# Seven-product feed-forward layers: 16 of 22 units cut, VectorE's second weight sum and gated product each one piece later

## The reference

```python
D_FF = -(-8 * D_MODEL // (3 * 256)) * 256      # 2816, that is 22 chunks of 128
def swiglu(x, w_gu, w_down):
    g, u = jnp.split(x @ w_gu, 2, axis=-1)
    return (jax.nn.silu(g) * u) @ w_down
...
h = h + swiglu(rms_norm(h, ffn_norm[layer]), ffn_w_gu[layer], ffn_w_down[layer])
```

## Time and profile before

| what | value |
|---|---|
| time, median of 3 runs | 2204.48 us (2204.3 to 2204.71) |
| the profiled execution: its time | 2204.36 us |
| its span in the trace | 2202.6 us |
| PE busy | 2166.3 us, 98% |
| DVE busy | 1304.2 us, 59% |
| ACT busy | 1015.8 us, 46% |
| first product stage of ffn0 | 504.85 to 577.15 us, first matmul of down |
| second product stage of ffn0 | 643.16 to 745.15 us, first matmul of down |

### The profile page before, as it was taken

How to read it: one execution, slowest core, us unless ns; L and a number is a source line. 1 busy time by engine, 2 the same in 40 slices (tenths; PEclk the granted TensorE clock), 3 DMA queues, 4 the chain that set the end, 5 groups by cost and what they waited for, 6 DMA issues and landing times.

```text
span 2202.6 us, 31009 instructions
## 1 busy us (share of the span) xinstructions
PE 2166.3 (98%) x11970; PEld 1819.5 (83%) x11970; DVE 1304.2 (59%) x1910; ACT 1015.8 (46%) x1516; POOL 308.2 (14%) x255
## 2 busy tenths in 40 slices
PE   8999999999999999999999999999999999999998
PEld 6888888789889888877898898878777778888887
DVE  6655656378658643554696486466576555555522
ACT  5445555345324434565453253355566554444312
POOL 0211112220000120003200000300010043222211
PEclk9999999999999999999999999999999999999999
DMA  3311111122323322201223223321221232222221
GB/s 139 115 58 39 56 41 39 58 96 77 117 83 108 115 96 77 96 20 53 83 80 131 77 99 132 134 91 44 72 73 39 72 111 95 101 95 95 96 96 58
DMA packets 31664, 184.79 MB, mean 84 GB/s; under 512 B 3105, under 2 KB 7713, under 8 KB 11313
## 3 DMA queue, kind: packets, MB, share of 16 engines
q1 hardware_dynamic: 29520, 175.42, 22.5%
q0 software_dynamic: 2016, 7.60, 1.1%
HBM read 178.78 MB, written 7.37 MB: 85 GB/s over the span
## 4 chain that ended last, share of the span: by engine, by line
PE 92%; DVE 4%; ACT 2%; issue 1%; DMA 0%; SPq 0%; POOL 0%; DVEq 0%; POOLq 0%; ACTq 0%
PE ps L2288 25%; PE ps L2290 25%; PE ps L2289 25%; PE ps L2618 2%; PE ps L3106 1%; PE ps L2612 1%; PE ps L3089 1%; PE ps L3049 1%; PE ps L2881 1%; PE ps L3116 1%; PE ps L2921 1%; PE ps L2639 1%; DVE wl L1221 0%; DVE sq L1977 0%; DMA raw<-in_stream 0%
## 5 line engine op out<-in xcount | busy, mean ns | idle before, releaser
L2288 PE MATMUL ps<-xh,wh 128*128 128x512 f32 (+1 forms) x1608 | 620.9, 386 | 3.3 <-POOL xl L2238 2.1
L2290 PE MATMUL ps<-xh,wl 128*128 128x512 f32 (+1 forms) x1608 | 595.1, 370 | 0.0
L2289 PE MATMUL ps<-xl,wh 128*128 128x512 f32 (+1 forms) x1608 | 593.9, 369 | 0.0
L1221 DVE TENSOR_TENSOR wl<-raw,wh 128x2048 fp32r<-128x2048 f32 x108 | 250.7, 2321 | 239.9 <-ACT wh L508 239.9
L2288 PEld LDWEIGHTS ps<-xh,wh 128*128 128x128 f32 x1608 | 303.6, 189 | 57.8 <-issue 11.9
L2290 PEld LDWEIGHTS ps<-xh,wl 128*128 128x128 f32 x1608 | 302.7, 188 | 53.2
L2289 PEld LDWEIGHTS ps<-xl,wh 128*128 128x128 f32 x1608 | 303.7, 189 | 47.6 <-issue 4.3
L508 ACT ACTIVATE wh<-raw 128x2048 fp32r<-128x2048 f32 x108 | 206.4, 1911 | 241.3 <-PE ps L2290 241.0
L2288 PE MATMUL ps<-part_h,wh 128*128 128x512 f32 x512 | 201.9, 394 | 0.5
L2290 PE MATMUL ps<-part_h,wl 128*128 128x512 f32 x512 | 200.6, 392 | 0.0
L2289 PE MATMUL ps<-part_l,wh 128*128 128x512 f32 x512 | 199.8, 390 | 0.0
(11 more groups left out here) (416 smaller groups left out, 3811.7 us busy)
## 6 DMA issues: line engine op xcount, KB each, us to landing
raw<-in_stream SPq DMA_DIRECT2D x158, 1024.0 KB, 4.8
hankd<-tabd SPq DMA_DIRECT2D x1, 3072.0 KB, 17.2
hank<-hankd POOLq DMA_DIRECT2D x4, 768.0 KB, 5.1
hT<-in_xT SPq DMA_DIRECT2D x4, 512.0 KB, 6.6
keepd<-hT POOLq DMA_DIRECT2D x1, 2048.0 KB, 9.9
hT<-keepd POOLq DMA_DIRECT2D x8, 256.0 KB, 4.8
out<-hT SPq DMA_DIRECT2D x8, 256.0 KB, 2.6
raw<-in_stream SPq DMA_DIRECT2D x2, 512.0 KB, 8.2
```

What stands on the lines that cost most here:

```text
L1221: dve.tensor_tensor(wl[:, s, :], raw[:, s, :], wh[:, s, :].bitcast(F32), ALU.subtract).then_inc(lo_made, 1)
L2288: pe.matmul(out, w_hi, a_hi, start=start, stop=False)
L2289: pe.matmul(out, w_hi, a_lo, start=False, stop=False)
L2290: return pe.matmul(out, w_lo, a_hi, start=False, stop=stop)
```

## The change

Both layers cut six units more in all, three each: the first stage has one uncut unit of its seven (5) in place of two (5 and 9), the second none of its ten in place of two (15 and 19). 16 of the 22 units of a layer are cut, before 13. The lists of skips (slots passed over) are new, so that the last piece of a unit and the following whole unit meet the slots that they need.

In the walk of the pieces, VectorE makes wsum[1] (second_operand) behind the low part of piece 1 and not ahead of it. The gated product of a unit stands one step later (p - 2 in place of p - 1), hidden on ScalarE one step later (p - 3 in place of p - 2), and hidden_lo on VectorE one step later (p - 4 in place of p - 3).

```diff
--- before.py
+++ after.py
@@ -109,7 +109,7 @@
 FAST = ("ffn0", "ffn1")
 PLAIN, CUT = 5, 12
 TOK = SEQ // 2
-GROUPS = ((PLAIN, CUT, "PSSSPSS", (20,)), (CUT, FC, "SSSPSSSPSS", ()))
+GROUPS = ((PLAIN, CUT, "PSSSSSS", (12, 13, 22, 23, 32, 33)), (CUT, FC, "SSSSSSSSSS", (30, 31)))
 CUTS = {n: kind == "S" for first, _, kinds, _ in GROUPS for n, kind in enumerate(kinds, first)}
 SEVENS = [n for n, cut in CUTS.items() if cut]
 QUARTERS = (7, 8, 9, 10)
@@ -656,7 +656,7 @@
 
                 def products(first, last):
                     order = pieces_of(first, last)
-                    for p in range(len(order) + 2):
+                    for p in range(len(order) + 3):
                         if p + LEAD < len(order):
                             hi(*order[p + LEAD])
                         n, k = order[p - 1] if 0 < p <= len(order) else (None, None)
@@ -664,12 +664,13 @@
                             copy_out(n)
                         elif k == 8:
                             silu_whole(n)
-                        n, k = order[p - 2] if p > 1 else (None, None)
+                        n, k = order[p - 2] if 1 < p <= len(order) + 1 else (None, None)
                         if k == 1:
                             silu_left(n)
                         elif k == 5:
                             silu_right(n)
-                        elif k in LAST:
+                        n, k = order[p - 3] if p > 2 else (None, None)
+                        if k in LAST:
                             hidden(n)
                         if p == len(order) - 3:
                             act.wait_ge(*piece_done(f, *order[-5]))
@@ -1419,7 +1420,7 @@
                     dve.wait_ge(operand_hi, fast_count(operand_hi, f, 3 * kc + 3))
                     dve.tensor_tensor(t_l[:, :, kc, :], t_sum, t_h[:, :, kc, :].bitcast(F32), ALU.subtract).then_inc(operand_lo, 1)
 
-                def first_sums(n):
+                def first_sum(n):
                     u, i = fast_unit(name, n), 4 * SEVENS.index(n)
                     q = [raw[:, u % 2, SEQ * j:SEQ * j + SEQ] for j in range(4)]
                     dve.wait_ge(raw_landed[u % 2], 16 * (u // 2) + 16)
@@ -1429,6 +1430,10 @@
                     else:
                         dve.wait_ge(operand_lo, fast_count(operand_lo, f, 12))
                     dve.tensor_tensor(wsum[:, 0, :], q[2], q[3], ALU.add).then_inc(weights_summed, 1)
+
+                def second_operand(n):
+                    u, i = fast_unit(name, n), 4 * SEVENS.index(n)
+                    q = [raw[:, u % 2, SEQ * j:SEQ * j + SEQ] for j in range(4)]
                     dve.wait_ge(weights_summed, fast_count(weights_summed, f, i + 1))
                     dve.tensor_tensor(wsum[:, 1, :], wsum[:, 0, :], q[0], ALU.subtract).then_inc(weights_summed, 1)
 
@@ -1455,12 +1460,14 @@
 
                 def operand(n, k):
                     if k == 1:
-                        first_sums(n)
+                        first_sum(n)
                     elif k == 2:
                         difference(n)
                     elif k == 3:
                         last_sum(n)
                     lo(n, k)
+                    if k == 1:
+                        second_operand(n)
 
                 def gate_left(n):
                     dve.wait_ge(prod_done, fast_count(prod_done, f, COUNT[n, 1]))
@@ -1494,7 +1501,7 @@
 
                 def products(first, last):
                     order = pieces_of(first, last)
-                    for p in range(len(order) + 3):
+                    for p in range(len(order) + 4):
                         if p + LEAD < len(order):
                             operand(*order[p + LEAD])
                         if p == len(order) - 3:
@@ -1512,10 +1519,10 @@
                             gate_right(n)
                         elif k == 6:
                             up_left(n)
+                        n, k = order[p - 2] if 1 < p <= len(order) + 1 else (None, None)
+                        if k in LAST:
                             gated(n)
-                        elif k == 10:
-                            gated(n)
-                        n, k = order[p - 3] if p > 2 else (None, None)
+                        n, k = order[p - 4] if p > 3 else (None, None)
                         if k in LAST:
                             hidden_lo(n)
```

## The result

| | before | after |
|---|---|---|
| time, median (runs) | 2204.6 us (4) | 2224.26 us (4), 2222.55 to 2225.24 |
| ratio, 95% interval | | 1.0089, 1.0076 to 1.0102 |
| profiled execution: time, span | 2204.36, 2202.6 us | 2225.24, 2223.4 us |
| mean granted TensorE clock | 0.999 | 0.994 |

Slower by 0.89%, where 2212.0 us (slower by 0.34%) was forecast: the direction holds, the time lies 6 us above the range.

What follows compares the result with a forecast made beforehand. TensorE, busy 98% of the span, was taken as the bound; per layer, longer waits of 4.05 and 2.6 us less 2.9 saved gave + 3.75, + 7.5 for two layers: 2212.0 us, range 2206.5 to 2218.

Steps and rivals of the forecast that it cites:

- The clock: Rival: TensorE's clock falls behind two stage-end waits (+ 3 us) or all four (+ 6), 2215 to 2219 us; chance 0.14.
- the forecast's own waits: TensorE waits before the down products: 4.4 us at each first stage end, 2.95 at each second.
- The prediction's last sign of being wrong: Granted TensorE clock behind the stage-end idles drops below 1.00 for long.
- VectorE's step: VectorE's time per cut unit: 10.28 us, between 10.1 and 10.46, falling 0.31 us behind TensorE each unit.
- The wait of 0.29 us for ScalarE: VectorE's wait within today's cut unit; moving ScalarE's copy behind silu_left should take most of it away.
- The chains at the stage ends: Product, silu_left, copy, split_hi, split_lo, then gate_right (first end) or hidden low part (second): waits 4.4 and 2.95 us.
- The bank shift: First stage end: with 44 results for 39, bank 4 holds (11, 5), so the down product waits for gate_right.
- TensorE's 9.97 us: Cut unit takes TensorE 9.97 us against 10.94 uncut, saving 2.9 us per layer, 5.8 in all.
- (d): Rival: TensorE runs dry inside the stages from late transfers or waits for ScalarE, + 1 to + 4 us more; chance 0.09.
- the margin at (11, 3): Thinnest place inside the first stage: piece made by 569.4, taken by TensorE at 570.2, 0.8 us left.
- (c): Rival: VectorE's time per cut unit comes down to 9.97 us; 2204.6 us, at best 2200.6; chance 0.15.

Runs made afterwards that it cites:

- experiment 2: Changed kernel with ScalarE's high part of the whole unit one step earlier, ahead of silu_left and hidden of the stage's last units: 2205.71 us, ratio 1.0006.
- experiment 3: Kernel before with the three moves in the operation order alone, still 13 cut units: 2208.76 us, ratio 1.002.
- experiment 4: Kernel before with the new table of 16 cut units alone, old order of VectorE's and ScalarE's operations: 2225.83 us, ratio 1.0093.
- experiment 6: Changed kernel with the whole unit's high part earlier on ScalarE and the bank rotation begun at bank 2 instead of 4: 2202.74 us, ratio 0.9993.
- experiment 9: Kernel before, with each down product's first matmul waiting for the stage's last hidden chunk, not the last but one: 2224.56 us, ratio 1.009.
- experiment 10: Changed kernel with ScalarE's high part for piece 1 of the next unit made ahead of silu_left and hidden: 2218.74 us, ratio 1.0062.
- experiment 11: Changed kernel with the bank rotation begun at bank 2 instead of 4, nothing else: 2221.81 us, ratio 1.0079.
- experiment 7: Changed kernel with the first weight sum made by GpSimd and not by VectorE: 2246.29 us, ratio 1.0189.
- experiment 8: Changed kernel with the whole unit's high part earlier, banks from 2, and the first weight sum on GpSimd: 2224.35 us, ratio 1.009.
- experiment 12: Changed kernel with the whole unit's high part earlier, banks from 2, and the next unit's piece 1 high part ahead of silu_left and hidden: 2199.15 us, ratio 0.9975.
- experiment 5: Changed kernel with 20 and 14 extra matmuls of ones on TensorE in the waits behind first and second stages: 2214.42 us, ratio 1.0046.
- experiment 1: Changed kernel with 36 and 24 extra matmuls of ones on TensorE behind the first and second stages: 2224.58 us, ratio 1.0091.

## Why the prediction was wrong

**The clock: the step that failed.** The sum had no term for it. It stood as a rival, 0.14, with 1.4 us per wait or up to twice that (1.5 to 2.9 were measured, so its price was about right), "against it that the new waits are shorter than 4.97, those of the second stage by 2 us". The start of the program is one case of an idle time that brings the lower clock, and I read its length as if it were a bound. It is none. The waits at the stage ends in the profiled runs of before, of the changed kernel and of experiments 2, 3, 4, 6, 9, 10 and 11, and what the slow steps behind them cost:

| wait, us | slow behind it | lost, us |
|---|---|---|
| 0.27 to 1.37 (14 waits) | none | 0 |
| 2.21 to 2.51 (6 waits) | two | 1.5, 1.6 |
| 3.43 to 3.66 (8 waits) | seven | 1.3 to 1.6 |
| 3.82 to 4.46 (6 waits) | all | 1.5 to 2.9 |
| 5.06, 5.08 | both | 2.7, 2.9 |

The four waits of experiment 7 (4.00 to 5.06 us) were all followed by slow steps too, those of 8 and 12 (1.38 at most) by none. Priced by this table, the forecast's own waits cost 3 to 9 us of clock: those of 4.35 us 1.5 to 2.9 each, those of 2.85, for which there is no row, 0 to 1.6 each. That is 2215 to 2221 instead of 2212. The falling clock was the likeliest case and not a rival. In the changed kernel it is 8.7 us in the trace, and experiment 5 shows that it goes when TensorE does not idle. The prediction's last sign of being wrong, the granted clock below 1.00 behind the idles, is the one that came. The Trainium skill, TensorE: Matmul & The Clock Gate, section Why this matters for your kernels, was cited for this and given too little weight; the trace agrees with it on every wait above 3.5 us. The page's limit for such gaps lies above two waits that were followed by slow steps here (2.41 and 2.51 us) and below one that was not (3.43); there the measurement decides.

**VectorE's step: a term mis-sized.** Taken as the middle of 10.1 and 10.46, which was a choice and no measurement; measured 10.39. The wait of 0.29 us for ScalarE went, as argued. But the low part of piece 1 now stands between the sums, and waits 0.13 us for its own high part, which ScalarE makes behind silu_left and hidden; another 0.16 stays before the low part behind up_left. Experiment 10 takes the first away. The first step of the first stage is longer still, 10.62 (523.80 to 534.42), with a wait of 0.31 us for ScalarE's high part at 529.67. The product of the last unit but one comes at 573.08 and not 572.3, and the waits are 5.07 and 3.62 (means of the two layers) where 4.35 and 2.85 were forecast: 3.0 us over four ends. So of the 13.3 us between the 2211.9 computed for the profiled execution and its 2225.24, 8.7 are the clock, 3.0 VectorE's lateness, and the rest lies where nothing was changed (see the ledger).

**The chains at the stage ends: right.** From split_lo's start to the down product 4.49 us (4.45 forecast), last waited gate_right at the first end; at the second end the hidden low part ends at 753.20, 0.22 before the down product starts (the trace names fork, right ahead of it). What the prediction did not say of them is how much of it was order: the high part of the whole unit behind silu_left and the copy costs 2.6 to 2.9 us at each end (experiment 2).

**The bank shift: right**, 1.1 to 1.2 us at each first end (experiment 11). **TensorE's 9.97 us: right**, ten units in 99.84 us (99.8 forecast). **Running dry inside the stages, (d): right that it hardly happens**, the margin at (11, 3) was used up to a gap of under 0.1 us. **VectorE keeps up, (c)**: not in the changed kernel. In experiment 12 its step of 10.24 is still above 9.97, but what it falls behind by no longer reaches TensorE at the second ends, since the other two parts of the waits are gone. Its 2199.15 us lie under the 2200.6 that (c) called the best the change can do, for (c) kept the order of the stage end as it was.

## What to carry to other kernels

Price a new wait of TensorE twice: its length, and the matmuls behind it at half clock, which in these runs cost 1.3 to 2.9 us more behind some waits of 2.4 us and behind all above 3.5; a clock that never falls in the trace of before says nothing on this when that trace has no such wait. A change that loads the second engine nearer to the first is paid where the pipeline drains: look there for the one operation in the wrong place of an in-order queue before giving up the saving. And an idle engine is not free help when its work slows the one that is full: time one operation of each side by side first.

## What the runs showed of the hardware

- The clock's answer to waits of equal length differs: of two waits of 2.51 and 2.47 us in one execution one was followed by slow steps, of four of 3.43 to 3.52 us three were. The times scatter accordingly: 2204.14 to 2208.13 us over eleven runs of experiment 2, 2198.09 to 2199.93 over nine of experiment 12. That the scatter is the clock's was not traced run by run.
- The slow steps need not begin with the first matmul: in the changed kernel the second down product starts at 753.42, four matmuls go at the full pace, and the slow steps run from 754.42 to 757.79.
- Matmuls of ones of 128 columns, whose results nobody reads, hold the clock at 1.00 through a wait (experiments 1 and 5). In experiment 5, where they end before the wait does, they cost nothing that the trace shows.
- In three of the 14 traces one down product ran at 0.2333 us per matmul to its end in place of 0.2289, at a granted clock of 1.00 (the changed kernel from 753.42 us on, experiment 4 from 582.24, experiment 10 from 750.00), 1.0 to 1.3 us each. All three had slow steps at their start; why only these stayed slower is open.
- VectorE's 0.68 us subtraction takes 1.73 us beside a GpSimd addition of 1.29 to 1.30 us, which itself is as fast as alone.
